# A transformer layer on one core: the adaLN sums on TensorE from pieces of w_ada, x turned in place, h made by VectorE

## The chip, the cores and the metric

The kernel runs on one core of a Trainium2 chip. The metric is the device time of one execution in microseconds (us). The engines are TensorE (PE, with its weight loads shown as PEld), VectorE (DVE), ScalarE (ACT), GpSimd (POOL) and SyncE (SP, which here only issues DMAs).

## The reference

One hybrid encoder layer on 512 tokens of width 1024: RMSNorm and adaLN conditioning, a wide projection `w_in` (1024 x 11264), dilated window attention and differential attention, gates, two projections, an output projection and a final norm. The change touches only its first lines:

```python
mod = jax.nn.silu(c) @ w_ada + b_ada               # c: (1, 1024), w_ada: (1024, 3072)
shift, scale, gate = jnp.split(mod, 3, axis=-1)
h = rms_norm(x, norm_pre) * (1.0 + scale[:, None]) + shift[:, None]
proj = h @ w_in
```

So `shift` and `scale` need the first 2048 columns of `w_ada`, 8 MB of float32, multiplied by one vector. `gate` is needed only at the end and is not touched. All data is float32.

## The kernel before

Large products are made in three passes of the type fp32r: each operand is cut into a high part and a rest (`h_hi`, `h_lo`, `w_hi`, `w_lo`), and hi x hi, lo x hi and hi x lo are added in PSUM (`PASSES`, `products`). The kernel holds h turned, that is with the 1024 features on partitions in KT = 8 pieces k of 128 features, each 128 x 512 tokens. The weights come in blocks of 256 columns, each block in two halves (a half is 4 pieces k, 512 KB); a half is loaded into one of three slots `raw`, ScalarE copies it to the high part (`cut_hi`) and GpSimd subtracts (`cut_lo`).

Every engine has its own instruction list written out by hand, and the engines meet at semaphores. An engine does its list strictly in order, so the order in the code is the order on the engine. The list after the start goes by "ticks" t from 8 on: projections of the next block, attention of the stage before and so on. Tiles 0 to 3 (q and k of the first stage) are made before tick 8, during the start, and the change is in this start.

The start before the change, piece by piece k = 0 to 7:

- SP loads c, x (4 tiles of 128 tokens) and, with `load_ada(k)`, piece k of the two needed thirds of `w_ada`: 1 MB in two DMAs, into one of two buffers `ada`. From k = 2 it waits for the sum that frees the buffer (`ada_used`). Halves 0 to 3 of `w_in` are loaded in between.
- ScalarE squares x with a sum per row (L764), GpSimd takes the power (L669), ScalarE and VectorE scale the four tiles of x (`x_in`, L779 and L1008).
- VectorE makes the sums: `sum_ada(k)` multiplies the eight 128 x 256 parts of the piece by silu(c) and adds them up into two partial sums `ada_sum` (L992 twice, L995 six times). TensorE adds them over the partitions, with `ada_sum` as stationary operand and a column of ones as moving operand (`modulation(k)`, L1478, 4 matmuls with one moving column), into PSUM bank `turned` or `sums`.
- VectorE makes `ab` (scale and shift of piece k) from it in three small operations (L1018 to L1020).
- TensorE turns piece k of x (`x_turn(k)`, L1489, 4 transposes) into one of two halves of the PSUM tensor `score`.
- ScalarE makes `h_f` and `h_hi` from `score` and `ab` (L790, L792), GpSimd makes `h_lo` (L674).
- TensorE adds piece k to tiles 0 to 3: 12 matmuls of 128 x 512 (L1457).

TensorE's list runs one piece ahead: `modulation(k + 1)`, `x_turn(k + 1)`, then the products of piece k. After piece 7 ScalarE copies the four tiles out (L804), SP swaps their halves for the rotary embedding by DMA (L565), and the ticks begin. The angles of the rotary embedding are computed by VectorE after piece 7 (L1033 to L1042); the masks by GpSimd after piece 3.

Of the kernel before, what the change touches and what calls it, by code (L numbers as in the profile page):

```python
# [20 lines left out]
ACT = mybir.ActivationFunctionType  # L21
# [113 lines left out]
def build(nc, x, c, positions, w_ada, b_ada, norm_pre, w_in, lambda_q1, lambda_k1, lambda_q2,  # L135
# [119 lines left out]
    with ExitStack() as ctx:  # L255
# [51 lines left out]
        ada = sb("ada", [P, 2, KT, 2, P], on=begin)  # L307
        ada_sum = sb("ada_sum", [P, 2, 2, 2, P], on=begin)
        h_f = sb("h_f", [P, 2, S], on=begin)
# [53 lines left out]
        ada_loaded = [sem(f"ada_loaded{i}") for i in range(2)]  # L363
# [26 lines left out]
        h_f_done = sem("h_f_done")  # L390
        h_hi_done = sem("h_hi_done")
# [25 lines left out]
        ada_added = sem("ada_added")  # L417
        ada_used = sem("ada_used")
# [78 lines left out]

        def yd_at(i, k):
            return yd[i][:, k, :] if k < 6 else yd_late[i][:, k - 6, :]
# [5 lines left out]
        def _(sp):  # L505
            def load_ada(k):
                if k >= 2:
                    sp.wait_ge(ada_used, 2 * (k - 1))
                src = w_ada[0].rearrange("(a p) n -> p a n", p=P)
                for i in range(2):  # L510
                    sp.dma_start(ada[:, k % 2, :, i, :],
                                 src[:, :, i * D + k * P:i * D + (k + 1) * P]).then_inc(ada_loaded[k % 2], 16)
# [10 lines left out]
            for tt in range(NT):  # L523
                if tt == 2:
                    load_ada(0)
                sp.dma_start(x_in[:, tt, :], x[0, tt * P:(tt + 1) * P, :]).then_inc(x_loaded[tt], 16)
            load_half(0)
            load_half(1)
            load_ada(1)
            load_ada(2)  # L530
            load_half(2)
            load_ada(3)
            load_half(3)
            for k in range(4, KT):
                load_ada(k)
# [81 lines left out]
        def _(pool):  # L617
# [52 lines left out]
            for half in prep_at(-1)[:2]:  # L670
                cut_lo(half)
            for k in range(KT):
                pool.wait_ge(h_hi_done, k + 1)
                nc.gpsimd.tensor_tensor(h_lo[:, k, :], h_f[:, k % 2, :], h_hi[:, k, :].bitcast(F32),  # L674
                                        ALU.subtract).then_inc(h_lo_done, 1)
                if k in (1, 2, 4, 6):
                    cut_lo(halves[2 + (1, 2, 4, 6).index(k)])
                if k == 3:
                    masks()
# [73 lines left out]
        def _(act):  # L753
# [24 lines left out]
            for tt in range(2, NT):  # L778
                nc.scalar.activation(x_in[:, tt, :], x_in[:, tt, :], ACT.Copy,  # L779
                                     scale=st[:, 8 + tt:9 + tt]).then_inc(x_norm_act, 1)  # L780
            for half in prep_at(-1)[:2]:
                cut_hi(half)


            for k in range(KT):
                act.wait_ge(x_turned, k + 1)
                act.wait_ge(ab_done, k + 1)
                if k >= 2:
                    act.wait_ge(h_lo_done, k - 1)
                nc.scalar.activation(h_f[:, k % 2, :], score[:, k % 2, :], ACT.Identity, bias=ab[:, 1, k:k + 1],  # L790
                                     scale=ab[:, 0, k:k + 1]).then_inc(h_f_done, 1)
                nc.scalar.activation(h_hi[:, k, :], score[:, k % 2, :], ACT.Identity, bias=ab[:, 1, k:k + 1],  # L792
                                     scale=ab[:, 0, k:k + 1]).then_inc(h_hi_done, 1)
                if k in (1, 2, 4, 6):
                    cut_hi(halves[2 + (1, 2, 4, 6).index(k)])
# [166 lines left out]
        def _(dve):  # L962
# [18 lines left out]
            link(tt_(silu_c[:, 1, :], silu_c[:, 0, :], cols[:, 0:KT], ALU.mult))  # L981

            def sum_ada(k):


                dve.wait_ge(ada_loaded[k % 2], 32 * (k // 2 + 1))
                if k >= 2:
# [585 lines left out]
```

## Time and profile before

| | |
|---|---|
| time, median of 3 runs | 973.95 us (973.0 to 983.67) |
| the profiled execution: its own time | 971.97 us |
| the profiled execution: span of the core | 970.1 us |
| PE busy | 844.4 us, 87% of the span |
| PEld / DVE / POOL / ACT busy | 700.0 / 545.8 / 418.0 / 358.0 us |
| mean granted clock of TensorE | 0.958 of full speed |
| DMA over the span | 94.76 MB, 98 GB/s |

Durations come from the profiled execution, whose time is 2 us below the median of the other runs. Times within it count from the start of the span. A group in an answer of the trace names the line, the engine, the operation, output <- inputs, shapes and a count; a matmul of float32 (not fp32r) with one moving column appears as two instructions, so the 4 matmuls of a `modulation(k)` are "x8". The granted clock 1.00 is 2.4 GHz and 0.50 is 1.2 GHz. The chain is the work that ended last, followed back from one releaser to the one before.

### The profile page before, as it was taken

To read this page: it belongs to the slowest core of one execution; us is meant where nothing else is said; L and a number is where in the kernel's file an instruction comes from. 1 tells how busy PE (TensorE), PEld (TensorE's weight loads), DVE (VectorE), ACT (ScalarE), POOL (GpSimd) and SP (SyncE) were. 2 spreads that over 40 slices of the span, in tenths; PEclk is the share of its full clock that TensorE was granted. 3 is DMA by queue.
4 is the path that set the end of the run, shared out by engine and by line. 5 is a ranking of instruction groups with operands and counts; after the bars stand their busy time and mean duration, and the time that the engine had idled before them with its cause. 6 is when DMAs were issued, how large, how long until landed. Compare 5 with 4: busy or idle time off the path is not lost.

```text
span 970.1 us, 12421 instructions
## 1 busy us (share of the span) xinstructions
PE 844.4 (87%) x4622; PEld 700.0 (72%) x4622; DVE 545.8 (56%) x881; ACT 358.0 (37%) x777; POOL 418.0 (43%) x309
## 2 busy tenths in 40 slices
PE   1588799999999999998878878887888898999897
PEld 1467588888888788886666657666766676888697
DVE  2877496664646464235777777767767664202222
ACT  3333353444353434333234334334425533322411
POOL 2465233433535353246655634133525415544910
PEclk9979799999999999999898989999989998999999
DMA  9763462222333332324322322112211203223512
GB/s 249 194 180 88 169 197 91 76 77 86 90 110 88 106 90 88 112 81 148 98 68 74 99 67 66 44 55 68 68 49 44 66 22 109 87 87 110 172 59 73
DMA packets 89715, 94.76 MB, mean 98 GB/s; under 512 B 5133, under 2 KB 80950, under 8 KB 89526
## 3 DMA queue, kind: packets, MB, share of 16 engines
q1 hardware_dynamic: 89360, 93.54, 31.6%
q0 software_dynamic: 240, 0.39, 0.4%
q8 instruction: 37, 0.61, 0.3%
q14 instruction: 24, 0.20, 0.1%
q10 hardware_dynamic: 54, 0.02, 0.0%
HBM read 78.11 MB, written 5.34 MB: 86 GB/s over the span
## 4 chain that ended last, share of the span: by engine, by line
PE 32%; DVE 28%; issue 11%; ACT 10%; POOL 7%; DMA 6%; SPq 4%; ACTq 0%; DVEq 0%; POOLq 0%
PE proj L1457 22%; DVE rope_o L1065 4%; PE proj L1540 3%; DVE dstat L1105 3%; ACT probs L858 3%; PE score L1336 2%; DVE dstat L1106 2%; DMA rope_s<-rope_x 2%; POOL w_lo L665 2%; SPq L546 2%; DVE probs L1123 2%; POOL rope_x L689 2%; DMA ada<-in_w_ada 2%; ACT at_hi L876 2%; DVE ada_sum L995 2%
## 5 line engine op out<-in xcount | busy, mean ns | idle before, releaser
L665 POOL TENSOR_TENSOR w_lo<-raw,w_hi 128x1024 fp32r<-128x1024 f32 x102 | 248.3, 2439 | 311.5 <-ACT w_hi L775 311.3
L1457 PE MATMUL proj<-h_hi,w_hi 128*128 128x512 f32 x608 | 257.6, 424 | 9.7 <-POOL h_lo L674 6.3
L1457 PE MATMUL proj<-h_lo,w_hi 128*128 128x512 f32 x608 | 244.9, 403 | 0.0
L1457 PE MATMUL proj<-h_hi,w_lo 128*128 128x512 f32 x608 | 244.0, 401 | 0.0
L1457 PEld LDWEIGHTS proj<-h_hi,w_hi 128*128 128x128 f32 x608 | 118.9, 196 | 48.2 <-issue 11.5
L1457 PEld LDWEIGHTS proj<-h_hi,w_lo 128*128 128x128 f32 x608 | 118.5, 195 | 27.3
L1457 PEld LDWEIGHTS proj<-h_lo,w_hi 128*128 128x128 f32 x608 | 119.3, 196 | 21.4
L775 ACT ACTIVATE w_hi<-raw 128x1024 fp32r<-128x1024 f32 x102 | 106.1, 1055 | 10.0 <-PE proj L1457 7.4
L689 POOL TENSOR_TENSOR rope_x<-rope_x,cos_t 128x512 f32<-128x512 f32 x36 | 55.6, 1544 | 105.4 <-DMA rope_s<-rope_x 105.3
L1353 PE MATMUL turned<-ident,probs 128*128 128x128 f32 x256 | 40.7, 283 | 45.5 <-DVE probs L1125 21.6
L1131 DVE TENSOR_TENSOR at_lo<-turned,at_hi 128x512 fp32r<-128x512 f32 x64 | 44.1, 689 | 62.6 <-ACT at_hi L876 62.2
L1382 PE MATMUL sums<-v,at_hi 128*128 128x128 f32 (+1 forms) x256 | 62.3, 313 | 16.2 <-DVE at_lo L1131 16.0
L1353 PEld LDWEIGHTS turned<-ident,probs 128*128 128x128 f32 x256 | 30.3, 143 | 59.8 <-issue 26.4
L858 ACT ACTIVATE probs<-score,dstat 128x512 f32<-128x512 f32 x64 | 43.5, 684 | 76.1 <-DVE dstat L1106 76.1
L866 ACT ACTIVATE probs<-score,rows_out 128x128 f32<-128x128 f32 (+1 forms) x96 | 37.6, 401 | 85.7 <-DVE rows_out L1115 85.7
L1382 PEld LDWEIGHTS sums<-v,at_hi 128*128 128x128 f32 x256 | 48.5, 190 | 23.0 <-DVE at_lo L1131 21.2
L1065 DVE TENSOR_TENSOR rope_o<-rope_x,rope_s 128x512 f32<-128x512 f32 (+2 forms) x38 | 51.7, 1365 | 15.7 <-POOL rope_x L689 14.8
L1384 PE MATMUL sums<-v,at_lo 128*128 128x64 f32 (+1 forms) x256 | 57.8, 234 | 0.0
L1457 PE MATMUL proj<-w_hi,h_hi 128*128 128x256 f32 x160 | 48.6, 304 | 1.9 <-ACT rope_x L804 1.9
L1384 PEld LDWEIGHTS sums<-v,at_lo 128*128 128x128 f32 x256 | 48.9, 191 | 1.3
L876 ACT ACTIVATE at_hi<-turned 128x512 fp32r<-128x512 f32 x64 | 38.0, 594 | 26.7 <-PE turned L1353 26.7
L1457 PE MATMUL proj<-w_lo,h_hi 128*128 128x256 f32 x160 | 46.9, 293 | 0.0
(236 smaller groups left out, 1611.6 us busy)
## 6 DMA issues: line engine op xcount, KB each, us to landing
raw<-in_w_in SPq DMA_DIRECT2D x88, 512.0 KB, 3.5
rope_s<-rope_x SPq DMA_DIRECT2D x144, 64.0 KB, 2.0
ada<-in_w_ada SPq DMA_DIRECT2D x16, 512.0 KB, 6.4
zd<-in_w_ada SPq DMA_DIRECT2D x8, 512.0 KB, 4.8
raw<-in_w_proj_b SPq DMA_DIRECT2D x8, 512.0 KB, 3.4
raw<-in_w_out SPq DMA_DIRECT2D x8, 512.0 KB, 3.4
rows_in<-window_rows SPq DMA_DIRECT2D x4, 792.0 KB, 4.5
window_rows<-rows_out SPq DMA_DIRECT2D x4, 528.0 KB, 3.4
```

Of the source, the lines that this page charges most:

```text
L665: nc.gpsimd.tensor_tensor(lo, raw[:, n % RAW, :, :], hi.bitcast(F32), ALU.subtract).then_inc(w_lo_done, 1)
L689: nc.gpsimd.tensor_tensor(at, at, cos_t[:], ALU.mult).then_inc(rope_cos_done, 1)
L775: nc.scalar.activation(w_place(half)[0], raw[:, n % RAW, :, :], ACT.Copy).then_inc(w_hi_done, 1)
L858: ins = nc.scalar.activation(probs[:, s.s % 2, i, :], score[:, i, :], ACT.Exp, bias=dstat[:, s.s % 2, i:i + 1], scale=SCALE, accum_out=dst ...
L866: ins = nc.scalar.activation(probs[:, s.s % 2, 0, i * w:(i + 1) * w], score[:, s.s % 2, i * w:(i + 1) * w], ACT.Exp, bias=rows_out[:, qt, ...
L876: nc.scalar.activation(at_hi[:, s.s % 2, :], turned[:], ACT.Copy).then_inc(t_hi_done, 1)
L1065: ins = tt_(dst, view(at), view(other), ALU.add)
L1131: tt_(at_lo[:, s.s % 2, :], turned[:], at_hi[:, s.s % 2, :].bitcast(F32), ALU.subtract).then_inc(t_read, 1)
L1353: ins = nc.tensor.transpose(turned[:, m * P:(m + 1) * P], probs[:, s.s % 2, 0, m * P:(m + 1) * P], ident[:])
L1382: mm(sums[:, to:to + 2 * width].rearrange("p (w e) -> p w e", w=2), hi[:, col:col + P], v[:, kt, :, col0:col0 + width], start=first, stop= ...
L1384: ins = mm(sums[:, to:to + width], lo[:, col:col + P], v[:, kt, 0, col0:col0 + width], start=False, stop=last, skip_group_check=True)
L1457: ins = mm(dst, left, right, start=k == 0 and n == 0, stop=k == nk - 1 and n == 2)
```

## The change

The sums over the rows of `w_ada` are made by TensorE alone: each 128 x 128 piece of `w_ada` is a stationary operand, the column of silu(c) is the moving operand, and eight of them are added in PSUM for each of scale and shift: 16 matmuls per k in place of 4. `sum_ada` and `ada_sum` are gone. `w_ada` comes in four chunks c_ of two pieces k each, 2 MB in four DMAs (runs of 1 KB in place of 512 B), into three buffers, and all of x is loaded ahead of it. Only the last chunk waits for a buffer.

All eight pieces of x are turned at the start and copied back from `score` into `x_in`, by ScalarE for even and by VectorE for odd k. h is then made in place in `x_in` by VectorE, `h_hi` by ScalarE and `h_lo` by VectorE in place of GpSimd. The masks and the angles are made earlier. TensorE's list is now, for each chunk: both modulations, then the products of both pieces.

```diff
@@ block.sync
+            def load_ada(c_):
+                if c_ == 3:
+                    sp.wait_ge(mod_done, 2)
...
+                for h in range(2):
+                    for i in (1, 0):
+                        at = i * D + c_ * 2 * P
+                        sp.dma_start(ada[:, c_ % 3, 4 * h:4 * h + 4, i, :],
+                                     src[:, 4 * h:4 * h + 4, at:at + 2 * P]).then_inc(ada_loaded[c_][h], 16)
             for tt in range(NT):
-                if tt == 2:
-                    load_ada(0)
                 sp.dma_start(x_in[:, tt, :], x[0, tt * P:(tt + 1) * P, :]).then_inc(x_loaded[tt], 16)
+            load_ada(0)
             load_half(0)
             load_half(1)
             load_ada(1)
+            load_half(2)
             load_ada(2)
-            load_half(2)
+            load_half(3)
             load_ada(3)
-            load_half(3)
-            for k in range(4, KT):
-                load_ada(k)
@@ block.gpsimd
-            for half in prep_at(-1)[:2]:
+            masks()
+            for half in prep_at(-1):
                 cut_lo(half)
-            for k in range(KT):
-                pool.wait_ge(h_hi_done, k + 1)
-                nc.gpsimd.tensor_tensor(h_lo[:, k, :], h_f[:, k % 2, :], h_hi[:, k, :].bitcast(F32),
...
@@ block.scalar
+            for k in range(0, KT, 2):
+                act.wait_ge(x_turned, k + 1)
+                nc.scalar.activation(x_cols(k), as_x(score[:, k % 2, :]), ACT.Copy).then_inc(x_back_act, 1)
             for half in prep_at(-1)[:2]:
                 cut_hi(half)
             for k in range(KT):
...
+                act.wait_ge(h_f_done, k + 1)
+                nc.scalar.activation(as_x(h_hi[:, k, :]), x_cols(k), ACT.Copy).then_inc(h_hi_done, 1)
+                if k in (3, 5):
+                    cut_hi(halves[2 + (3, 5).index(k)])
+            for half in prep_at(-1)[4:]:
+                cut_hi(half)
@@ block.vector
-                for kk in range(KT):
-                    part = ada_sum[:, k % 2, kk % 2]
...
+            for k in range(1, KT, 2):
+                dve.wait_ge(x_turned, k + 1)
+                nc.vector.tensor_copy(x_cols(k), as_x(score[:, k % 2, :])).then_inc(x_back_dve, 1)
+
+            def modulate(k):
                 mod = (turned, sums)[k % 2]
...
+                ts_(x_cols(k), x_cols(k), ab[:, 0, k:k + 1], ab[:, 1, k:k + 1], ALU.mult, ALU.add).then_inc(h_f_done, 1)
+
+            def h_cut(k):
+                dve.wait_ge(h_hi_done, k + 1)
+                tt_(as_x(h_lo[:, k, :]), x_cols(k), as_x(h_hi[:, k, :]).bitcast(F32), ALU.subtract).then_inc(h_lo_done, 1)
+
+            for c_ in range(4):
+                modulate(2 * c_)
+                modulate(2 * c_ + 1)
+                h_cut(2 * c_)
+                h_cut(2 * c_ + 1)
...
@@ block.tensor
-                    for part in range(2):
-                        ins = mm((turned, sums)[k % 2][:, i:i + 1], ada_sum[:, k % 2, part, side, :], ones[:, 0:1],
-                                 start=part == 0, stop=part == 1)
+                for kk in range(KT):
+                    if kk % 4 == 0:
+                        pe.wait_ge(ada_loaded[c_][kk // 4], 32)
+                    for i, side in enumerate((1, 0)):
+                        ins = mm(bank[:, i:i + 1], ada[:, c_ % 3, kk, side, (k % 2) * P:(k % 2 + 1) * P],
+                                 silu_c[:, 1, kk:kk + 1], start=kk == 0 and i == 0, stop=kk == KT - 1,
+                                 skip_group_check=True)
...
+            for k in range(6):
+                x_turn(k)
+            modulation(0)
+            x_turn(6)
+            x_turn(7)
+            modulation(1)
+            for c_ in range(4):
+                if c_:
+                    modulation(2 * c_)
+                    modulation(2 * c_ + 1)
+                for k in (2 * c_, 2 * c_ + 1):
+                    pe.wait_ge(h_lo_done, k + 1)
+                    for tile in tiles[:4]:
+                        products(tile, [k])
```

TensorE at the start of the program, before (`turned` and `sums` hold the modulation, `score` the turned x, `proj` the products):

```order
L1467 MATMUL sums<-ident,rows 128x41
L1478 MATMUL turned<-ones,ada_sum 128x1 x4
L1489 MATMUL score<-ident,x_in 128x128 x4
L1478 MATMUL sums<-ones,ada_sum 128x1 x4
L1489 MATMUL score<-ident,x_in 128x128 x4
L1457 MATMUL proj<-h_hi,w_hi 128x512
```

And TensorE at the same place now:

```order
L1459 MATMUL sums<-ident,rows 128x41
L1488 MATMUL score<-ident,x_in 128x128 x24
L1474 MATMUL turned<-silu_c,ada 128x1 x16
L1488 MATMUL score<-ident,x_in 128x128 x8
L1474 MATMUL sums<-silu_c,ada 128x1 x16
L1449 MATMUL proj<-h_hi,w_hi 128x512
```

All eight turns and 32 one-column matmuls now stand ahead of the first product, where two turns and 8 such matmuls stood.

TensorE between the products of pieces 1 and 2, before:

```order
L1457 MATMUL proj<-h_hi,w_lo 128x512
L1478 MATMUL sums<-ones,ada_sum 128x1 x4
L1489 MATMUL score<-ident,x_in 128x128 x4
L1457 MATMUL proj<-h_hi,w_hi 128x512
```

And there now:

```order
L1449 MATMUL proj<-h_hi,w_lo 128x512
L1474 MATMUL turned<-silu_c,ada 128x1 x16
L1474 MATMUL sums<-silu_c,ada 128x1 x16
L1449 MATMUL proj<-h_hi,w_hi 128x512
```

Four matmuls with one moving column and a turn stood between the products of any two pieces; now 32 such matmuls stand between pairs of pieces and nothing inside a pair.

VectorE's list for the first chunk, now (`x_in` holds the turned x and then h; `ab` is scale and shift):

```order
L991 COPY x_in<-score 128x4x128 x4
L997 TENSOR_TENSOR ab<-turned,cols 128x1
L998 TENSOR_SCALAR ab<-ab,cols 128x1
L999 TENSOR_TENSOR ab<-turned,cols 128x1
L1005 TENSOR_SCALAR x_in<-x_in,ab 128x4x128
L997 TENSOR_TENSOR ab<-sums,cols 128x1
L998 TENSOR_SCALAR ab<-ab,cols 128x1
L999 TENSOR_TENSOR ab<-sums,cols 128x1
L1005 TENSOR_SCALAR x_in<-x_in,ab 128x4x128
L1009 TENSOR_TENSOR h_lo<-x_in,h_hi 128x512 x2
```

The rests `h_lo` of both pieces stand behind the modulation of the second, so the first product of a chunk waits for both of its modulations.

## Rows read from the trace of the kernel before

**Rows 1.** Busy time of each engine by stretch, granted clock, DMA share and rate.

```profile
core 0: us, PE busy (x) PEld busy (x) DVE busy (x) ACT busy (x) POOL busy (x), PEclk, DMA share, GB/s
0.00:20.00 20.00, 1.05 (x5) 0.84 (x5) 3.58 (x11) 5.92 (x10) 4.88 (x16) 1.00 0.91 245
...
40.00:60.00 20.00, 15.56 (x81) 12.53 (x81) 18.15 (x39) 5.29 (x7) 11.38 (x17) 0.91 0.74 198
60.00:80.00 20.00, 17.61 (x74) 14.12 (x75) 15.35 (x33) 8.13 (x12) 9.89 (x6) 0.83 0.43 133
...
120.00:240.00 120.00, 117.70 (x716) 98.87 (x717) 79.53 (x104) 51.95 (x132) 40.32 (x20) 1.00 0.35 109
```

**Rows 2.** Chain that ended last, in order of time: start, us, what.

```profile
45.25 5.53 DVE ada_sum L995 x6
...
76.93 3.07 PE proj L1457 x12
80.03 0.61 ACT zd L804
```

**Rows 3.** Timeline of ScalarE at the start: start, us, engine, line, operation.

```profile
7.26 1.06 ACT L764 ACTIVATE gate_row<-x_in 128x1024 f32<-128x1024 f32 x1 [0.23 <-DMA x_in<-in_x]
...
19.02 1.06 ACT L764 ACTIVATE gate_row<-x_in 128x1024 f32<-128x1024 f32 x1 [0.18 <-DMA x_in<-in_x]
...
21.53 2.19 ACT L779 ACTIVATE x_in<-x_in,st 128x1024 f32<-128x1024 f32 x2 [1.36 <-POOL st L669]
```

**Rows 4.** Timeline of TensorE: one-column matmuls, turns, products, at both clocks.

```profile
33.11 1.84 PE L1478 MATMUL sums<-ones,ada_sum 128*128 128x1 f32 x8 [8.17 <-DVE ada_sum L995]
34.81 1.09 PE L1489 MATMUL score<-ident,x_in 128*128 128x128 f32 x4
35.56 0.78 PE L1457 MATMUL proj<-h_hi,w_hi 128*128 128x512 f32 x1
...
49.34 0.63 PE L1457 MATMUL proj<-h_hi,w_lo 128*128 128x512 f32 x1
49.76 0.63 PE L1457 MATMUL proj<-h_hi,w_hi 128*128 128x512 f32 x1
...
52.10 0.95 PE L1478 MATMUL turned<-ones,ada_sum 128*128 128x1 f32 x8
52.91 0.63 PE L1489 MATMUL score<-ident,x_in 128*128 128x128 f32 x4
...
54.57 0.40 PE L1457 MATMUL proj<-h_lo,w_hi 128*128 128x512 f32 x1
54.81 0.40 PE L1457 MATMUL proj<-h_hi,w_lo 128*128 128x512 f32 x1
```

**Rows 5.** Stretches in which, or after which, the granted clock changes.

```profile
65.46:68.88 3.42, 2.38 (x17) 2.00 (x16) 3.32 (x8) 0.13 (x1) 2.42 (x2) 1.00 0.36 94
68.88:72.29 3.41, 3.41 (x10) 2.66 (x9) 0.34 (x3) 2.26 (x3) 2.02 (x2) 0.50 0.17 60
...
106.30:113.20 6.90, 6.83 (x21) 5.33 (x22) 1.74 (x3) 3.64 (x7) 4.67 (x2) 0.50 0.37 111
...
659.40:662.80 3.40, 1.47 (x7) 0.87 (x5) 2.37 (x5) 2.21 (x5) 2.64 (x2) 1.00 0.51 154
```

**Rows 6.** Timeline of VectorE: modulation, operations of 128 x 512.

```profile
73.36 0.16 DVE L1018 TENSOR_TENSOR ab<-sums,cols 128x1 f32<-128x1 f32 x1 [4.10 <-PE sums L1478]
...
73.88 0.42 DVE L1033 CAST rope_x<-merged 128x512 f32<-128x512 int32 x1
74.33 0.49 DVE L1034 TENSOR_SCALAR rope_x<-rope_x,rope_c 128x512 f32<-128x512 f32 x1
...
93.54 0.68 DVE L1072 TENSOR_TENSOR q_lo<-rope_o,q_hi 128x512 fp32r<-128x512 f32 x1
```

**Rows 7.** Costliest groups of the page: cutting of one weight half.

```profile
L665 POOL TENSOR_TENSOR w_lo<-raw,w_hi 128x1024 fp32r<-128x1024 f32 x102 | 248.3, 2439 | 311.5 <-ACT w_hi L775 311.3
...
L775 ACT ACTIVATE w_hi<-raw 128x1024 fp32r<-128x1024 f32 x102 | 106.1, 1055 | 10.0 <-PE proj L1457 7.4
```

More of the change, by code:

```diff
@@ L306, in build @@
         x_in = sb("x_in", [P, NT, D], on=begin)
-        ada = sb("ada", [P, 2, KT, 2, P], on=begin)
-        ada_sum = sb("ada_sum", [P, 2, 2, 2, P], on=begin)
-        h_f = sb("h_f", [P, 2, S], on=begin)
+        ada = sb("ada", [P, 3, KT, 2, 2 * P], on=begin)
         rows = sb("rows", [P, P], on=begin)
@@ L362, in build @@
         x_loaded = [sem(f"x_loaded{i}") for i in range(NT)]
-        ada_loaded = [sem(f"ada_loaded{i}") for i in range(2)]
+        ada_loaded = [[sem(f"ada_loaded{c_}_{i}") for i in range(2)] for c_ in range(4)]
         raw_loaded = [sem(f"raw_loaded{i}") for i in range(RAW)]
@@ L980, in _ @@
             link(ts_(silu_c[:, 0, :], silu_c[:, 0, :], 0.5, 0.5, ALU.mult, ALU.add))
[L981 to L987, printed above, removed]
-                    dve.wait_ge(mod_done, k - 1)
-                for kk in range(KT):
-                    part = ada_sum[:, k % 2, kk % 2]
-                    if kk < 2:
-                        ins = ts_(part, ada[:, k % 2, kk], silu_c[:, 1, kk:kk + 1], None, ALU.mult)
-                    else:
-                        dve.wait_ge(ada_added, 6 * k + kk - 1)
-                        ins = stt(out=part, in0=ada[:, k % 2, kk], scalar=silu_c[:, 1, kk:kk + 1],
-                                  in1=part, op0=ALU.mult, op1=ALU.add)
-                    if kk < KT - 2:
-                        ins.then_inc(ada_added, 1)
-                    else:
-                        ins.then_inc(ada_used, 1)
-            sum_ada(0)
+            tt_(silu_c[:, 1, :], silu_c[:, 0, :], cols[:, 0:KT], ALU.mult).then_inc(silu_done, 1)
+            dve.wait_ge(rows_turned, 2)
+            dve.wait_ge(silu_done, 1)
+            nc.vector.tensor_copy(cols[:, KT:41], sums[:, KT:41]).then_inc(cols_done, 1)
             dve.wait_ge(act_x_sq, NT)
@@ L1008, in _ @@
                 ts_(x_in[:, tt, :], x_in[:, tt, :], st[:, 8 + tt:9 + tt], None, ALU.mult).then_inc(x_norm_done, 1)
-            dve.wait_ge(rows_turned, 2)
-            nc.vector.tensor_copy(cols[:, KT:41], sums[:, KT:41]).then_inc(cols_done, 1)
-            dve.wait_ge(cols_done, 2)
-            for k in range(KT):
-                if 0 < k < KT - 1:
-                    sum_ada(k + 1)
+            for k in range(1, KT, 2):
+                dve.wait_ge(x_turned, k + 1)
+                nc.vector.tensor_copy(x_cols(k), as_x(score[:, k % 2, :])).then_inc(x_back_dve, 1)
+            def modulate(k):
                 mod = (turned, sums)[k % 2]
+                dve.wait_ge(cols_done, 2)
                 dve.wait_ge(mod_done, k + 1)
@@ L1490, in x_turn @@
                 ins.then_inc(x_turned, 1)
+            for k in range(6):
+                x_turn(k)
             modulation(0)
-            x_turn(0)
-            for k in range(KT):
-                if k + 1 < KT:
-                    modulation(k + 1)
-                    x_turn(k + 1)
-                pe.wait_ge(h_lo_done, k + 1)
-                for tile in tiles[:4]:
-                    products(tile, [k])
+            x_turn(6)
[9 more added lines that the diff above has]
+                        products(tile, [k])
             running = by_tick(tiles[4:], lambda t: t.first)
```

84 lines of the change are left out of this document (38 added, 46 removed).

## The prediction

> **What bounds the kernel now.** I read the busy time by stretches first. From 120 us on TensorE is busy 117.7 of 120 us; only the first 80 us leave it idle, 1.05 of 20 us at first and 15.56 and 17.61 of 20 later [rows 1]. The change works there, so I ask when the products of piece 7 end. In the chain that is 76.93 + 3.07 = 80.0 us, and ScalarE's copy of the tiles starts at 80.03 [rows 2]. Everything later hangs on that copy and on a full TensorE behind it [rows 1, 2], so I take a shift of this end, which I call T, to reach the end of the kernel one to one. Before T the pace was VectorE's: it is busy 18.15 of 20 us from 40 to 60 [rows 1], and its adding up of `ada_sum` is in the chain, 5.53 us for six operations [rows 2]. The DMAs had room: 0.74 and 0.43 of their time, 198 and 133 GB/s against 245 at the start [rows 1].
>
> **The change, part by part.** VectorE loses all 64 operations of `sum_ada`. TensorE gets 16 one-column matmuls per piece in place of 4, two instructions each: 32 a piece, 256 in all where there were 64.
>
> *Price of one such instruction.* With the slow clock eight of them start at 33.11 and the next work at 34.81: 1.70 / 8 = 0.2125 us. With the fast clock 52.10 to 52.91: 0.81 / 8 = 0.101, and I take 0.106, half of the slow price [rows 4]. So a piece costs 6.8 us slow or 3.4 us fast, and all eight 54.4 or 27.1 us. A product of 128 x 512 takes 49.76 - 49.34 = 0.42 (0.427) slow and 54.81 - 54.57 = 0.24 (0.23 on average) fast; the 24 of a chunk 10.2 or 5.5 us. Four turns take 35.56 - 34.81 = 0.75 us slow [rows 4].
>
> The Trainium skill (TensorE: Matmul & The Clock Gate, section LDWEIGHTS) prices a weight load of 128 columns at 107 ns with no word of the clock. By it all 256 would take 27.4 us in either state. Rows 4 agree at the fast clock only, and the measured 0.2125 decides for the slow one.
>
> *Which clock.* This decides the case. In the stretch 65.46 to 68.88 TensorE was busy 2.38 of 3.42 us, but with eight one-column instructions, four turns and only the beginning of a group of products; the clock fell to 0.50 right behind it. From 659.4 to 662.8 it was busy only 1.47 of 3.40 us, all with full products, and the clock was not lowered in that stretch [rows 5]. So time spent in one-column matmuls seems to hold the clock up little or not at all. Now 64 of them stand in a row between two groups of products. I take it that the clock falls during them in every chunk.
>
> *How long each clock lasts.* The products of a piece ended at about 65.4 and the clock stayed up until 68.88, 3.4 us [rows 5]; I take 3.6 us behind each group of products, with 3.4 and 4.6 as the two ends (the upper end is my estimate, one more third). For the way back, slow stretches full of products lasted 3.4 and 6.9 us [rows 5]; I take 4.3, nearer the short one since these products are dense from the start, and keep 3.4 and 6.9 as the ends.
>
> *One chunk.* The sums: 3.6 us fast hold 34 instructions, the other 30 take 6.4 us: 10.0 us (9.1 to 10.2). Then TensorE waits for VectorE: three small operations for `ab`, 73.36 to 73.88, 0.5 us; h in place, 0.5; the rest of the first piece, 0.68 [rows 6]; with 0.15 for the hand-overs 1.85 us. (ScalarE cuts the first piece during the second modulation.) The products: 4.3 us slow hold 10, the other 14 take 3.2: 7.5 us (7.1 to 8.7). Together 19.35 us (18.1 to 20.8).
>
> *One more wait.* The second block's half for pieces 4 to 7 is cut only behind `h_hi` of piece 5: 0.5 + 0.5 + 0.7, then 1.05 on ScalarE and 2.44 on GpSimd [rows 6, 7] and 0.2 of hand-overs, 5.4 us after the sums end. The products reach it after 1.85 + 6 x 0.427 = 4.4 us. So 1.0 us once.
>
> *The front.* x now goes ahead of `w_ada`. Tile 1 was squared at 7.26, tile 3 only at 19.02, behind 1 MB of `w_ada` [rows 3]. Two more tiles of 0.5 MB at 245 to 300 GB/s (the first rate is that of the start [rows 1], the second an estimate above it) are 3 to 4 us, so tile 3 at 10.3 (9.5 to 12). From that square to x scaled went 21.53 + 2.19 - 19.02 = 4.7 us [rows 3]: 15.0. Six turns with copies between them (0.75 each against 0.6 to 0.8 of copying on two engines in turn), 0.92 each: 20.5. Nothing has raised the clock by then, so slow: modulation 0 6.8, 27.3; two turns, 29.1; modulation 1, 35.9; wait 1.85; products 7.5: 45.25. The masks on GpSimd and the first two weight cuts (2 x 2.44 [rows 7], from about 30 on) are hidden by the turns and by modulation 1, and cost 1 to 2 us if the clock is fast there. The 2 + 8 + 2 MB to be loaded take 51 us at 245 GB/s and the last chunk is wanted at 85, so loads are hidden; its wait for modulation 1 (35.9) costs nothing either, though the second of the halves behind it on SP waits too. Angles and masks made earlier save nothing: the chain does not run through them [rows 2]. GpSimd's eight `h_lo` move to VectorE, inside the 1.85.
>
> *Sum.* T = 45.25 + 3 x 19.35 + 1.0 = 104.3 us against 80.0: 24.3 us later. The profiled execution took 971.97 us, so 996.3; its time is 2.0 below the median of 973.95, so **998 us** beside that median, 2.5% slower. With all low ends T is 44.9 + 3 x 18.1 + 1 = 100, with all high ends 46.5 + 3 x 20.8 + 1 = 110: 994 to 1004.
>
> **The rivals.**
>
> *B, the clock stays up.* If weight loads back to back do count as work, TensorE has hardly a gap and is fast from the first sums on. T = 20.5 + 3.4 + 1.3 + 3.4 + 1.85 + 5.5 = 36.0, three chunks of 6.8 + 1.85 + 5.5 = 14.15, and the wait for the half grows to 5.4 - 1.85 - 1.4 = 2.1: 80.6. That is 0.6 us later, 974.5 us. For it: TensorE's rows would be nearly unbroken. Against: the busy 2.38 us before the fall [rows 5]. This is also what the Trainium skill would have (TensorE: Matmul & The Clock Gate, section Why this matters for your kernels: keep TensorE busy without gaps and it runs at full clock). The same page (Part 4, PE-mode transpose) excepts turns only, and says nothing of one-column matmuls.
>
> *Between.* They count in part, and some chunks stay fast: T about 95, 989 us.
>
> *C, faster.* In bursts of eight the spacing may be that of starting and ending the burst, and 64 in a row may run closer. Beside B's clock, half the price, 0.053 us, gives 256 x 0.053 = 13.6 us less: T = 67, 961 us. It decides from a spacing under about 0.066 us on, where T falls by more than 1% of the time below 80. Against it: 0.2125 and 0.101 are in the proportion of the two clocks [rows 4], as a price per column would be, not one of a burst.
>
> *D, worse.* The slow clock, and VectorE's operations stretched by GpSimd's cuts, 2 us in each chunk, or a slow stretch of 6.9 us in each: 1006 to 1010 us.
>
> **How the numbers follow.** The slow-clock case 0.76 (994 to 1004), between 0.05, B 0.12, C 0.04, D 0.03. The time is that of the first. The range goes from 984 to 1010 and holds the first, the one between and D; B and C stay out with 0.16. A measurement of this kernel can tell about 1% from no change, that is 10 us. Faster by over 1% is C, 0.04; within 1% is B, 0.12; slower is the rest, 0.84.
>
> **What would show it.** Right: the ending of piece 7's products near 104 us; the groups of one-column matmuls at a mean spacing near 0.16 us, fast first and then slow in each chunk; a granted clock of 0.50 in part of every chunk and a mean under 0.85 from 40 to 100; VectorE idle more than half of 40 to 100; no wait for `ada` behind 40 us; behind T the same chain as before, 24 us later. Wrong: a granted clock of 1.00 throughout the sums (B), a spacing under 0.07 us (C), TensorE waiting for a load in chunks 1 to 3, or a shift of T that is not found at the end.

## The result, and the profile after

| | before | after |
|---|---|---|
| time, median of 4 runs each | 973.48 us (971.8 to 983.67) | 999.14 us (996.41 to 1000.49) |
| ratio, 95% interval | 1 | 1.022 (1.018 to 1.027) |
| profiled execution: time / span | 971.97 / 970.1 us | 998.28 / 996.5 us |
| mean granted clock of TensorE | 0.958 | 0.935 |
| PE / DVE / POOL busy | 844.4 / 545.8 / 418.0 us | 881.9 / 526.0 / 408.4 us |

The changed kernel is slower, by 2.2% as the ratio has it (between 1.8 and 2.7%). The two medians of the table alone would give 1.026. The time is 1 us above the predicted 998 and inside the range.

Line numbers in this part are those of the changed kernel: one-column matmuls L1474, turns L1488, products L1449, h in place L1005, `h_lo` L1009, `h_hi` L788, copies of the turned x L991 and L783, ScalarE's copy of the finished tiles L801, weight rests L672.

Busy time by stretch of the changed kernel, the same columns as [rows 1]:

```profile
core 0: us, PE busy (x) PEld busy (x) DVE busy (x) ACT busy (x) POOL busy (x), PEclk, DMA share, GB/s
0.00:20.00 20.00, 3.48 (x15) 2.83 (x16) 3.23 (x8) 8.87 (x13) 10.04 (x29) 1.00 0.91 265
...
40.00:60.00 20.00, 18.06 (x90) 16.46 (x89) 8.37 (x20) 2.21 (x3) 1.74 (x1) 0.67 0.23 77
60.00:80.00 20.00, 18.05 (x89) 15.92 (x87) 3.98 (x15) 2.21 (x3) 2.45 (x2) 0.67 0.09 27
80.00:100.00 20.00, 17.54 (x88) 15.58 (x88) 3.52 (x11) 3.25 (x5) 1.61 (x2) 0.67 0.09 27
```

From 40 to 80 us TensorE is busier than in [rows 1] (18.06 and 18.05 of 20 us against 15.56 and 17.61), and VectorE, which set the pace before with 18.15 of 20, works 8.37 and then 3.98. But the granted clock is 0.67 where it was 0.91 and 0.83, and this state lasts for 20 us more. The chain that ended last, in order of time (start, us, what), shows the chunks one behind the other:

```profile
17.09 3.85 PE score L1488 x16
22.37 4.56 PE turned L1474 x32
28.73 6.63 PE sums L1474 x32
37.30 7.73 PE proj L1449 x24
45.03 3.46 PE turned L1474 x32
48.49 6.81 PE sums L1474 x32
57.23 7.98 PE proj L1449 x24
65.21 3.46 PE turned L1474 x32
68.67 6.54 PE sums L1474 x32
80.59 6.87 PE proj L1449 x18
87.46 3.47 PE turned L1474 x32
90.92 5.04 PE sums L1474 x32
97.89 8.16 PE proj L1449 x24
```

Products end at 45.03, 65.21, 87.46 and 97.89 + 8.16 = 106.05 us. In [rows 2] the products of piece 7 ended at 80.0, so T moved by 26.05 us. The span grew by 26.4. What the slow clock cost can be estimated from these rows: the 256 one-column instructions took 39.97 us where 256 x 0.106 are 27.1, and the 96 products took 7.73 + 7.98 + 9.80 + 8.16 = 33.7 us (chunk 2 without its wait of 0.52) where 96 x 0.23 are 22.1. That makes about 24 us, so with the clock always up the products would have ended near 82, about where they ended before.

Below, T is compared by the end of ScalarE's copy of the four tiles, the same instruction group in every kernel. Its row in the two kernels:

```profile
77.94 2.68 ACT L804 ACTIVATE zd<-proj 128x512 f32<-128x512 f32 x4 [2.36 <-PE proj L1457]
```

```profile
104.01 2.66 ACT L801 ACTIVATE zd<-proj 128x512 f32<-128x512 f32 x4 [4.12 <-PE proj L1449]
```

It ends at 80.62 before and 106.67 after. From there to the end of the span are 889.5 us before and 889.8 after: the shift of the start reaches the end one to one.

### The profile page after: what moved, and what is told of

Its sections match the earlier page's. It is cut to its first block, busy times and chain, and to the rows that moved or that the text cites. A ratio compares the mean times of both kernels' runs of the same rounds, so it can differ in the third digit from the quotient of the medians.

```text
span 996.5 us, 12751 instructions
## 1 busy us (share of the span) xinstructions
PE 881.9 (89%) x4814; PEld 737.6 (74%) x4814; DVE 526.0 (53%) x837; ACT 354.2 (36%) x773; POOL 408.4 (41%) x301
## 4 chain that ended last, share of the span: by engine, by line
PE 37%; DVE 26%; issue 11%; ACT 10%; POOL 7%; DMA 5%; SPq 3%; ACTq 0%; DVEq 0%; POOLq 0%
PE proj L1449 22%; DVE rope_o L1057 5%; PE proj L1544 3%; DVE dstat L1097 3%; DMA rope_s<-rope_x 3%; ACT probs L855 3%; SPq L553 3%; PE sums L1474 3%; POOL rope_x L689 2%; POOL w_lo L672 2%; PE score L1328 2%; DVE dstat L1098 2%; DVE probs L1115 2%; PE turned L1474 2%; ACT at_hi L873 1%
## 5 line engine op out<-in xcount | busy, mean ns | idle before, releaser
L672 POOL TENSOR_TENSOR w_lo<-raw,w_hi 128x1024 fp32r<-128x1024 f32 x102 | 249.0, 2445 | 358.5 <-ACT w_hi L775 358.4
L1449 PE MATMUL proj<-h_hi,w_hi 128*128 128x512 f32 x608 | 260.6, 429 | 11.2 <-DVE h_lo L1009 7.8
L1449 PE MATMUL proj<-h_lo,w_hi 128*128 128x512 f32 x608 | 248.3, 408 | 0.0
L1449 PE MATMUL proj<-h_hi,w_lo 128*128 128x512 f32 x608 | 247.7, 407 | 0.0
L1449 PEld LDWEIGHTS proj<-h_hi,w_hi 128*128 128x128 f32 x608 | 121.4, 200 | 49.9 <-issue 11.4
L1449 PEld LDWEIGHTS proj<-h_hi,w_lo 128*128 128x128 f32 x608 | 120.6, 198 | 28.0
L1449 PEld LDWEIGHTS proj<-h_lo,w_hi 128*128 128x128 f32 x608 | 121.3, 200 | 22.5
L1057 DVE TENSOR_TENSOR rope_o<-rope_x,rope_s 128x512 f32<-128x512 f32 (+2 forms) x38 | 53.7, 1418 | 15.7 <-POOL rope_x L689 14.8
L1376 PE MATMUL sums<-v,at_lo 128*128 128x64 f32 (+1 forms) x256 | 57.8, 234 | 0.0
L1449 PE MATMUL proj<-w_hi,h_hi 128*128 128x256 f32 x160 | 48.0, 300 | 2.2 <-ACT rope_x L801 2.2
L1449 PE MATMUL proj<-w_hi,h_lo 128*128 128x256 f32 x160 | 46.4, 290 | 0.0
```

Of the source, the lines that this page charges most:

```text
L672: nc.gpsimd.tensor_tensor(lo, raw[:, n % RAW, :, :], hi.bitcast(F32), ALU.subtract).then_inc(w_lo_done, 1)
L1057: ins = tt_(dst, view(at), view(other), ALU.add)
L1376: ins = mm(sums[:, to:to + width], lo[:, col:col + P], v[:, kt, 0, col0:col0 + width], start=False, stop=last, skip_group_check=True)
L1449: ins = mm(dst, left, right, start=k == 0 and n == 0, stop=k == nk - 1 and n == 2)
```

## The experiments

### Which clock: sums between products, and useless products between sums

In the changed kernel TensorE still has a gap of 1.94 us in each chunk, and the clock falls. Two causes could be meant: the gap and the 64 one-column instructions in a row, or the one-column matmuls themselves. `e1_spread` issues exactly the same instructions, but the sums of the next chunk stand between the products of this one, so that the gap is gone too. Each call of `between()` issues two one-column matmuls (four instructions), behind each of the first 16 of 24 products.

```diff
                         ins = mm(dst, left, right, start=k == 0 and n == 0, stop=k == nk - 1 and n == 2)
+                        if between is not None:
+                            between()
...
             for c_ in range(4):
-                if c_:
-                    modulation(2 * c_)
-                    modulation(2 * c_ + 1)
```

> The changed kernel with the same instructions in another order on TensorE: the 32 one-column matmuls (64 instructions) of chunk c_+1 are set between the products of chunk c_, two behind each of the first 16 of 24 products. Nothing is left out. Theory A (the clock falls because one-column matmuls in a row do not hold it up; products between them do): chunks 0 to 2 take 5.5 + 6.8 = 12.3 us each at the fast clock, the first some 2 us more for its slow beginning, the last 5.5, and VectorE's 1.9 us behind the sums is hidden behind the last 8 products. The products of piece 7 end near 84 instead of 106 us: 976 us, granted clock near 1.00 from 45 us on, two slow rows at most. Rival B (the slow clock belongs to the start of this kernel, to its loads or to the share of time that TensorE is busy, whatever the order): only the 3 x 1.9 us of waiting go away, end near 100, 993 us. Rival C (one-column matmuls between products break their pipelining): each costs over 0.2 us, end past 106.

`e3_filler` leaves the changed kernel as it is, but puts two useless products behind every four one-column instructions of chunks 1 to 3, 96 in all. Their result goes to a bank that nobody reads at that time.

```diff
+                    if c_:
+                        for _ in range(2):
+                            mm(score[:, 0, :], w_hi[:, 0, 0, 0:P], h_hi[:, 0, :], start=True, stop=True)
```

> The changed kernel with 96 useless products of 128 x 512 added (into the free bank score), two behind every four one-column matmul instructions of chunks 1 to 3. TensorE has 7.4 us more work at the fast clock in each of these chunks (13.7 at the slow one). Theory A (clock): the sums of a chunk take 6.8 + 7.4 = 14.2 us at the fast clock, where they took 10.4 half slow, and the products behind them 5.5 where they took 7.9: 21.6 us a chunk against 20.3, end near 111 us, 1002 to 1006 us, and the clock stays up behind 45 us. Rival B (the clock does not depend on what stands between): 7.4 to 13.7 us more a chunk, end at 128 to 147 us, 1020 us or more.

`e1_spread` took 1004.3 us (median of 4, 995.73 to 1010.75; ratio to before 1.024, 1.017 to 1.031); its copy of the tiles ended at 114.26 us. Its profiled execution is the longest of the four, so I read the start from it and not the time. Busy time by stretch of e1_spread:

```profile
40.00:60.00 20.00, 20.00 (x75) 17.98 (x74) 6.34 (x17) 2.21 (x3) 1.22 (x1) 0.50 0.19 60
60.00:80.00 20.00, 20.00 (x79) 18.56 (x79) 1.24 (x6) 0.63 (x1) 1.14 (x1) 0.50 0.09 27
80.00:100.00 20.00, 20.00 (x74) 17.97 (x74) 3.82 (x14) 2.21 (x3) 2.36 (x1) 0.50 0.09 27
```

and three steps of TensorE's timeline in it (start, us, engine, line, operation):

```profile
49.83 0.85 PE L1476 MATMUL sums<-silu_c,ada 128*128 128x1 f32 x4
50.54 0.77 PE L1449 MATMUL proj<-h_hi,w_hi 128*128 128x512 f32 x1
51.11 0.85 PE L1476 MATMUL sums<-silu_c,ada 128*128 128x1 f32 x4
```

TensorE is busy for 20.00 of 20 us, three times over, at the lower of its two clocks. The period is 51.11 - 49.83 = 1.28 us, which is 4 x 0.2125 + 0.427. With 16 of them and eight bare products of 0.427 a chunk takes 23.9 us, against 20.18 and 22.25 of the changed kernel with its gaps. I had expected products to end near 84 us. The gap is hidden as meant, and the kernel is no faster, so the waiting was not what kept the clock low; in the changed kernel, too, the clock fell at 48.4 us, in the middle of the sums and 7 us before the wait. Each one-column instruction costs its slow price of 0.2125 us here and no more, so broken pipelining (the rival C of the expectation) is not the reason. Busy share isn't the measure of the clock either: here it is 1.

`e3_filler` took 1011.07 us (one run); the copy ended at 112.71. Its stretches:

```profile
40.00:60.00 20.00, 18.63 (x114) 16.07 (x113) 6.06 (x16) 2.12 (x3) 0.00 (x0) 1.00 0.18 58
60.00:80.00 20.00, 19.59 (x118) 16.86 (x116) 2.08 (x10) 0.72 (x2) 2.40 (x1) 1.00 0.09 27
80.00:100.00 20.00, 18.53 (x100) 15.56 (x101) 3.21 (x12) 2.21 (x3) 2.35 (x1) 0.91 0.09 27
```

With 96 x 0.23 = 22 us of work added, T came only 6.0 us later, because the clock was at 1.00, 1.00 and 0.91 where it had been 0.67. So one-column matmuls in a row don't hold the clock up, and with two full products behind every four instructions it stays up. It still fell twice before T, at 80.7 and 104.6 us, and both times inside a wait of TensorE for `h_lo`. The first of them:

```profile
80.96 0.80 PE L1449 MATMUL proj<-h_hi,w_hi 128*128 128x512 f32 x1 [1.37 <-DVE h_lo L1009]
```

A wait of the same 1.37 us at 57.8 did not bring it down, so waits may cost the clock where the mixture alone does not, but not each time. Its time is longer than T explains: from the copy to the end are 896.6 us where the changed kernel has 889.8. That stays open; later parts of other profiled executions differ by as much (table below).

`e1_spread` has four one-column instructions to a product at a clock that was low from the start. It doesn't tell whether the mixture can't raise the clock or can't hold it. `e7_spread_late` begins the mixture only behind 12 full products, with the clock up, has one or two matmuls behind a product instead of always two, and puts a useless product behind each of the sums left over.

```diff
+                def between():
+                    n_products[0] += 1
+                    n = n_products[0]
+                    if c_ == 0 and n <= 12:
+                        return
+                    for _ in range(2 if n % 3 == 0 else 1):
+                        next(steps_, None)
```

> The changed kernel with the one-column matmuls spread as before between products (four per three products), but only from the 13th product of chunk 0 on, when the clock is already up; the 16 matmuls (32 instructions) of piece 3 that find no product of chunk 0 get a useless product each. The first spread run showed that the mixture never raises the clock: 85 us at 1.2 GHz with TensorE busy all the time. Theory A2 (a mixture that can't raise the clock can still hold it once it is up): 6.2 + 7.1 us behind the first 12 products, then 1.95 + 12.3 us for chunks 1 and 2 and 1.95 + 5.5 for the last: end of piece 7 at 88 to 92 us, 980 to 984 us, granted clock 1.00 from 40 to 90 us. Rival A3 (the mixture neither raises nor holds it): from chunk 1 on 24 us a chunk, end near 115 us, 1007 us.

It took 1009.57 us (median of 4, 1008.54 to 1010.47; ratio 1.031, 1.027 to 1.035), and the copy ended at 114.44. Stretches of e7_spread_late, first the 12 products of chunk 0 with 32 one-column instructions between them, then the 32 left over with 16 useless products, then chunks 1 and 2:

```profile
39.73:45.74 6.01, 6.01 (x45) 5.57 (x43) 2.74 (x6) 0.00 (x0) 0.00 (x0) 1.00 0.59 188
45.74:53.00 7.26, 7.26 (x50) 6.57 (x49) 1.07 (x4) 0.63 (x1) 0.00 (x0) 1.00 0.00 0
56.00:100.00 44.00, 42.05 (x156) 37.93 (x156) 5.04 (x19) 2.84 (x4) 4.60 (x2) 0.50 0.08 25
```

and the first product of chunk 1:

```profile
54.84 0.51 PE L1449 MATMUL proj<-h_hi,w_hi 128*128 128x512 f32 x1 [1.60 <-DVE h_lo L1009]
```

The time is that of rival A3, its mechanism only in part. The mixture did hold a clock that was up, for 13.3 us (39.73 to 53.00), the first 6 us of it in the same proportion as in chunks 1 and 2. The clock fell at 55.5 us, behind a wait of 1.60 us and only 0.6 us into the mixture of chunk 1; whether it would have held without that wait, no run tells. Once down, the mixture did not raise it, though TensorE was busy for 42.05 of 44 us: it rose at 110.1, in the last chunk's products with nothing between them.

### What the sums cost, and what the rest gives

`e2_one_part` leaves out seven of the eight parts of each sum, so `scale` and `shift` are not the reference's and 32 of the 256 one-column instructions remain. All else is the changed kernel.

```diff
                     for i, side in enumerate((1, 0)):
+                        if kk < KT - 1:
+                            continue
```

> The changed kernel with seven of the eight parts of each sum over w_ada left out (4 one-column instructions a piece in place of 32); all loads and waits for them stay, so the output is another. It shows what the rest of the change is worth when the sums cost nothing. Theory A (the sums on TensorE and the clock that they cost are the whole loss): chunks of 1.9 + 5.5 + 0.4 = 7.8 us from about 25 us on, end of piece 7 at 55 to 58 us, 948 to 951 us, faster than the kernel before by 23 us or more; clock up after the first products. Rival (something else in the change is late, a load or VectorE's in-place h): the end stays above 75 us and a wait for ada or for x_in shows.

963.09 us (one run, before 977.56 on that chip), the copy ended at 71.77. The sums, but for the eighth left in, are worth 106.67 - 71.77 = 34.9 us of T, and the rest of the change would gain 80.62 - 71.77 = 8.9 if the sums cost no more than that eighth. I had expected less than 60 us. The waits of e2_one_part on its first 106 us (engine, line, releaser: us in total, times, longest) say what is there instead:

```profile
PE proj L1449 <- DVE h_lo L1009: 14.4, 4, 6.6
```

With nothing left between two pairs of products TensorE waits 2.59 us in each later chunk for VectorE, ScalarE and VectorE in turn, 6.65 before the first, and the clock is 0.83 and not 1.00 from 40 to 80. In the 6.65 us VectorE makes h of the first two pieces in 2.58 and 1.94 us where it takes 0.55 later on, while GpSimd cuts weights (rival D of the prediction, here on the critical path).

`e5_sums_alone` is the other half: the kernel before, one piece at a time, with only its sums made by TensorE.

```diff
-                if 0 < k < KT - 1:
-                    sum_ada(k + 1)
...
-                for i, side in enumerate((1, 0)):
-                    for part in range(2):
-                        ins = mm((turned, sums)[k % 2][:, i:i + 1], ada_sum[:, k % 2, part, side, :], ones[:, 0:1],
+                for kk in range(KT):
+                    for i, side in enumerate((1, 0)):
+                        ins = mm((turned, sums)[k % 2][:, i:i + 1], ada[:, k % 2, kk, side, :], silu_c[:, 1, kk:kk + 1],
```

> The kernel before with one part of the change alone: the sums on TensorE (16 one-column matmuls a piece, 32 instructions), VectorE's 64 operations gone; loads by piece in two buffers, order on TensorE, h on ScalarE and GpSimd as before. Theory A: each piece is 32 one-column instructions, a turn, 12 products; only 3.3 us of it count for the clock, so it goes up and down: 8 to 11 us a piece from about 26 us on, end of piece 7 near 100 us (92 to 112), 985 to 1003 us. Rival B (one-column matmuls hold the clock): 6.7 us a piece, end near 82 us, 976 us. If it is slower than before by as much as the changed kernel, the sums alone carry the loss.

992.14 us (one run, same before), copy at 98.52, as expected: 17.9 us later than before.

`e4_dve_sums` is the changed kernel with its sums back on VectorE, of pairs of pieces; all eight turns stand ahead of the first sums, and the angles behind the last piece again.

```diff
                 modulate(2 * c_)
+                if c_ < 3:
+                    sum_ada(2 * c_ + 2)
                 modulate(2 * c_ + 1)
                 h_cut(2 * c_)
                 h_cut(2 * c_ + 1)
+                if c_ < 3:
+                    sum_ada(2 * c_ + 3)
```

> The changed kernel with one part undone: the sums go back to VectorE (64 operations of 128 x 256 in ada_sum, 8 one-column instructions a piece on TensorE); load order, chunks, all turns first and h on VectorE stay; the angles go behind the last piece again. Theory A (sums on TensorE are the loss, the rest of the change is a gain): VectorE needs 3.5 + 0.6 + 0.5 + 0.7 = 5.3 us a piece from about 22 us on, 43 us, some 8 us more where GpSimd's cuts hold it up, then the last pair of products: end of piece 7 at 72 to 80 us instead of 106.7 (80.6 before), 965 to 973 us, same or a little faster than before. Rival (the new order itself is late, the products of two pieces wait for both sums): end past 85 us, 978 us or more.

984.14 us (median of 10; ratio 1.006, 1.003 to 1.009), copy at 85.73; products were expected to end at 72 to 80. Again the wait for the rests of h, in e4_dve_sums:

```profile
PE proj L1480 <- DVE h_lo L1036: 16.0, 4, 5.0
```

A sum of the next pair stands ahead of `h_lo` in VectorE's list, and TensorE waits four times; it also waits 8.0 us at the front for the first sum. With the sums taken off TensorE, T is still 5.1 us later than before, so the new order by pairs is late in itself, as the rival of the expectation had it. The two halves, 17.9 and 5.1, make 23.0 of the 26.05 measured.

### A version that divides the sums

`e6_split`, made from e4_dve_sums, lets VectorE make six of the eight parts and TensorE two, and puts the sums of piece k + 2 directly behind the products of piece k.

```diff
-NV = 8
+NV = 6
...
                 for k in (2 * c_, 2 * c_ + 1):
...
                         products(tile, [k])
+                    if k + 2 < KT:
+                        modulation(k + 2)
```

> As the run with VectorE's sums, but two of the eight parts of each sum are added by TensorE straight from w_ada (16 one-column instructions a piece in place of 8 or 32), VectorE adds six parts (2.6 us in place of 3.5), and on TensorE the sums of piece k+2 stand behind the products of piece k, not in pairs. Theory A: VectorE 4.4 us a piece, TensorE 1.7 + 2.8 = 4.5 us: end of piece 7 at 65 to 73 us, 957 to 966 us, faster than both kernels. Rival (TensorE's clock stays down since products and waits alternate): 6.8 + 1.9 us a piece on TensorE, end near 90 us, 982 us.

983.12 us (median of 10; ratio 1.005, 1.001 to 1.008), copy at 86.93, where products were expected to end at 65 to 73 us. TensorE's order was by piece now, VectorE's still by pair, and so were the waits, four of 1.95 us. Waits of e6_split:

```profile
PE turned L1511 <- DVE ada_sum L1010: 6.3, 1, 6.3
PE proj L1480 <- DVE h_lo L1036: 7.8, 4, 1.9
PE proj L1480 <- POOL w_lo L676: 1.9, 1, 1.9
```

`e8_by_piece`, made from e6_split, changes VectorE's list to the same order, and has the half for pieces 4 to 7 cut behind piece 3.

```diff
-                modulate(2 * c_)
-                if c_ < 3:
-                    sum_ada(2 * c_ + 2)
-                modulate(2 * c_ + 1)
-                h_cut(2 * c_)
-                h_cut(2 * c_ + 1)
-                if c_ < 3:
-                    sum_ada(2 * c_ + 3)
+                for k in (2 * c_, 2 * c_ + 1):
+                    modulate(k)
+                    if k + 2 < KT:
+                        sum_ada(k + 2)
+                    h_cut(k)
```

> The split run with VectorE's list by piece, not by pair: scale and h of piece k, six parts of the sum of piece k+2, then the rest of piece k, so that the products of a piece no longer wait for the next piece's sum, and the wait for ScalarE's high part is covered by the sum; and the second block's half for pieces 4 to 7 is cut behind piece 3, not 5 (it held TensorE up by 1.9 us). Theory (in the split run TensorE lost four times 1.95 us to the pairs, 1.9 to the half, and ran slow behind each of these gaps): 1.7 + 2.8 us a piece on TensorE without gaps from about 35 us on, the first products slow: end of piece 7 at 70 to 76 us instead of 86.9, 960 to 968 us, 1% faster than before. Rival (VectorE, stretched by GpSimd's cuts, is the pace: 2.3 + 0.6 + 0.55 + 0.7 us a piece, and the clock falls in the gaps it leaves): end near 80 us, 970 to 975 us, same as before.

972.31 us (median of 10, before 980.01 on the same chip; ratio 0.994, 0.990 to 0.998), copy at 74.69. T is where it was expected, the time is not (960 to 968). This is the first version ahead of the kernel before, by 0.6% with an interval from 0.2 to 1.0%. Its waits and its stretches:

```profile
PE proj L1477 <- DVE h_lo L1036: 1.8, 2, 1.2
```

```profile
40.00:60.00 20.00, 18.81 (x109) 16.52 (x108) 16.19 (x44) 3.47 (x5) 4.56 (x2) 0.93 0.36 114
60.00:80.00 20.00, 19.24 (x117) 16.77 (x116) 14.03 (x27) 6.82 (x10) 4.92 (x2) 0.96 0.23 67
```

The waits for `h_lo` went from 7.8 to 1.8 us, the clock is 0.93 and 0.96, and VectorE is used again (16.19 and 14.03 of 20 us). What remains at the front is the first sum, which TensorE awaits for 6.4 us. `e9_sum_first`, e8_by_piece otherwise, puts it ahead of VectorE's copies of the turned x.

```diff
+            sum_ada(0)
             for k in range(1, KT, 2):
                 dve.wait_ge(x_turned, k + 1)
                 nc.vector.tensor_copy(x_cols(k), as_x(score[:, k % 2, :])).then_inc(x_back_dve, 1)
-            sum_ada(0)
```

> As the run by piece, with the sum of piece 0 ahead of VectorE's four copies of x and not behind them. In the split run VectorE was idle from about 16.5 to 18 us and its first sum took 6.4 us (22.4 to 28.8), 4 of them behind GpSimd's first two cuts. Theory (the first sum is what the first products wait for): the first products begin 3 to 5 us earlier, end of piece 7 at 66 to 72 us, 956 to 964 us. Rival (the first chunk of w_ada lands only at 18 to 20 us, so the sum delays the copies and with them the turns by as much as it gains): same as the run by piece within 2 us.

974.36 us (median of 12; ratio 0.994, 0.990 to 0.998), copy at 75.87: the same as e8_by_piece within 2.1 us, as its rival expected. The wait moved:

```profile
PE score L1521 <- DVE x_in L1016: 3.1, 1, 3.1
PE sums L1508 <- DVE ada_sum L1006: 4.5, 1, 4.5
```

TensorE now waits 3.1 us in its turns for the copies behind the sum, and then 4.5 for the second sum.

All kernels side by side; "rest" is the span of the profiled execution less the end of the copy, and the mean ratio is against the runs of before on the same chip:

| kernel | copy ends | rest | median (runs) | ratio |
|---|---|---|---|---|
| before | 80.62 | 889.5 | 973.48 (4) | 1 |
| after | 106.67 | 889.8 | 999.14 (4) | 1.022 |
| e1_spread | 114.26 | 894.6 | 1004.3 (4) | 1.024 |
| e2_one_part | 71.77 | 889.5 | 963.09 (1) | |
| e3_filler | 112.71 | 896.6 | 1011.07 (1) | |
| e4_dve_sums | 85.73 | 896.4 | 984.14 (10) | 1.006 |
| e5_sums_alone | 98.52 | 891.8 | 992.14 (1) | |
| e6_split | 86.93 | 889.6 | 983.12 (10) | 1.005 |
| e7_spread_late | 114.44 | 893.5 | 1009.57 (4) | 1.031 |
| e8_by_piece | 74.69 | 890.0 | 972.31 (10) | 0.994 |
| e9_sum_first | 75.87 | 899.9 | 974.36 (12) | 0.994 |

The rest lies between 889.5 and 900 us, so one run tells the time to about 1%. T does not contain this rest, but comes from one profiled execution of each kernel, and how far it differs from one execution to the next was not measured. Why the rest differs was not looked into. The order of the kernels by T is nearly that by time.

## Why the prediction was right

**The verdict and its cause.** TensorE took over 256 one-column instructions, the clock fell during them in each chunk, and T moved by 26.05 us against 24.3 predicted. The clock was the disputed step: the trace of before had two stretches for it [rows 5], and e1 and e3 tested it directly: the same sums with the gap hidden left the clock at 0.50, and useless full products among them kept it at 1.00. By the estimate above T would be near 82 with the clock always up, which is what rival B had (80.6).

**Price of one instruction.** Predicted 0.2125 and 0.106 us. The fast 32 at 44.87 take 48.35 - 44.87 = 3.48 us, 0.109 each; the slow 32 of modulation 1 take 6.83, 0.213 each. The mean over the 256 of the chain is 39.97 / 256 = 0.156; "near 0.16" was predicted. Rival C, a closer spacing in long rows, is excluded. Where the Trainium skill (TensorE: Matmul & The Clock Gate, section LDWEIGHTS) gives 107 ns for 128 columns with no word of the clock, the 0.109 of the fast clock agrees and the measured 0.213 at the slow clock decides, as in [rows 4].

**The front.** Predicted end of the first products 45.25, measured 45.03, but by two errors that nearly cancel. The last tile of x was squared at 12.24 and not at 10.3, just past the high end of the range given (12). ScalarE's rows at the start:

```profile
12.24 1.06 ACT L764 ACTIVATE gate_row<-x_in 128x1024 f32<-128x1024 f32 x1 [2.43 <-DMA x_in<-in_x]
...
14.75 2.19 ACT L779 ACTIVATE x_in<-x_in,st 128x1024 f32<-128x1024 f32 x2 [1.36 <-POOL st L676]
```

So the turns began at 17.09 instead of 15.0. Against it, "nothing has raised the clock by then" was wrong. TensorE's timeline at the front:

```profile
17.09 4.42 PE L1488 MATMUL score<-ident,x_in 128*128 128x128 f32 x20 [11.84 <-ACT x_in L779]
21.71 0.66 PE L1488 MATMUL score<-ident,x_in 128*128 128x128 f32 x4 [0.20 <-DVE x_in L991]
22.20 4.72 PE L1474 MATMUL turned<-silu_c,ada 128*128 128x1 f32 x32
26.79 1.95 PE L1488 MATMUL score<-ident,x_in 128*128 128x128 f32 x8
28.53 6.83 PE L1474 MATMUL sums<-silu_c,ada 128*128 128x1 f32 x32
37.30 0.79 PE L1449 MATMUL proj<-h_hi,w_hi 128*128 128x512 f32 x1 [1.94 <-DVE h_lo L1009]
```

Modulation 0 took 4.6 us where 32 slow instructions take 6.83, so it ran partly at the fast clock, behind nothing but turns. The granted clock of the rows can't be read here, since it stands at 1.00 from the beginning, also over slow turns; the durations decide.

**The wait in each chunk.** 1.85 predicted, 1.93 to 1.95 measured ([1.94 <-DVE h_lo L1009] above).

**The chunks.** 19.35 each, and 1.0 once, were predicted for chunks 1 to 3. Measured: 20.18, 22.25 and 18.59, together 61.0 against 59.05, within the 18.1 to 20.8 given but for chunk 2. The term that was mis-sized is how long the slow clock lasts into the products. In chunk 2 the wait for the second block's half came as named and cost 0.52 us (1.0 predicted), but the clock rose only at about 85.9, 8.8 us into the products (4.3 taken, 6.9 the high end). Its stretches and rows around the wait:

```profile
77.10:84.00 6.90, 6.34 (x14) 4.56 (x15) 1.22 (x6) 1.00 (x2) 2.36 (x1) 0.50 0.25 76
84.00:87.30 3.30, 3.30 (x12) 2.56 (x12) 0.00 (x0) 0.00 (x0) 0.00 (x0) 0.70 0.00 0
```

```profile
80.59 0.80 PE L1449 MATMUL proj<-h_hi,w_hi 128*128 128x512 f32 x1 [0.52 <-POOL w_lo L672]
...
85.45 0.63 PE L1449 MATMUL proj<-h_hi,w_lo 128*128 128x512 f32 x1
85.87 0.43 PE L1449 MATMUL proj<-h_hi,w_hi 128*128 128x512 f32 x1
```

In chunks 0, 1 and 3 the clock rose 4.3, 4.8 and 5.1 us into the products. Why it rose late in chunk 2 is open: the wait of half a microsecond stands there, but e2_one_part and e3_filler have the same wait (0.61 and 0.51 us) in their chunk 2 and the clock rose 3.5 and 3.2 us into the products. Behind the products the clock lasted 3.4, 3.7 and 5.3 us (3.6 taken, 4.6 the high end); the 5.3 made chunk 3 the short one. Two readings of [rows 5] under these terms were loose: the clock did not stay up until 68.88 through the products before it, it had risen only at 65.5, at their end; and in the 6.9 us from 106.30 the first 2.8 are score matmuls of the attention, not products. The sum came close because a long stretch in chunk 2 and a short one in chunk 3 partly cancelled.

**The rest.** VectorE was idle for more than half of 40 to 100, as predicted, and no wait for `ada` came behind 40 us. The shift of T was found at the end (26.05 and 26.4), though TensorE was not as full behind T as the prediction had it: before the change it was busy 17.29 and 13.77 of 20 us from 80 to 120.

**The rivals.** B (clock stays up) fell: 0.67 in place of 1.00. D, VectorE stretched by GpSimd, was there in one place only, and hidden: h of piece 0 took 2.17 us beside GpSimd's cuts where it otherwise takes 0.55, but during modulation 1. VectorE's timeline:

```profile
30.01 2.17 DVE L1005 TENSOR_SCALAR x_in<-x_in,ab 128x512 f32<-128x512 f32 x1
...
36.09 0.55 DVE L1005 TENSOR_SCALAR x_in<-x_in,ab 128x512 f32<-128x512 f32 x1
```

## What to carry to other kernels

Before work is moved to TensorE, look at what kind of matmul it becomes: a float32 matmul of 128 x 128 weights with one moving column is two instructions of 0.106 us at the fast clock, together nearly the 0.23 of a product of 512 columns, and such matmuls in a row let the clock fall for the real products behind them as well. Dividing the sums between two engines, with both lists in the same order piece by piece, gave the only two versions here ahead of the kernel before, by 0.6%. When a busy engine gets slower, read its granted clock beside its busy share, since a share of 20.00 of 20 us can be had at half speed.

## What the runs showed of the hardware that was not expected

- TensorE can be busy for 82.06 of the 84 us from 24 to 108 (20.00 of 20 in three stretches) with a granted clock of 0.50 all along, where 16 of 24 products have four one-column instructions behind them (e1_spread). With 32 such instructions among 12 products a clock that was up stayed up (6.01 us, and 7.26 more with 16 products among 32); behind a wait of 1.60 us it fell, and the same mixture did not bring it back (e7_spread_late).
- The clock was up behind turns in a row, 24 of 128 x 128 with small waits between them: the 32 one-column instructions behind them took 4.6 us, not 6.8. Nothing in the trace of before showed this.
- Adding 22 us of useless products to a start that waits on TensorE cost 6 us (e3_filler).
- What the rest of the change is worth depends on where the sums are made: with an eighth of the sums the new order gained 8.9 us, with the sums on VectorE in pairs it lost 5.1, with the sums divided and by piece it gained 80.62 - 74.69 = 5.9.
